# Early heads' out projection moved between the last head's steps, the first up block in other PSUM banks, and two last steps of a stage moved

## The chip, the cores and the metric

The kernel runs on one core of one Trainium2 chip. The metric is device time in microseconds (us), the median of three runs. Engine names: PE is TensorE (matmuls), PEld its weight loads, ACT is ScalarE, DVE is VectorE, POOL is GpSimd, SP is the engine that here only issues the weight loads.

## The reference, cut to what matters

The program is three transformer layers in float32 over 256 tokens of width 2048. Layer norms follow each part.

```python
# layer 0: pooling mixer, then MLP; layer 1: dilated attention, then MLP
h = pool_mixer(x, ...)  or  dilated_attention(x, w_qkv, w_out)
x = layer_norm(ALPHA * x + h, ...)
x = layer_norm(ALPHA * x + relu(x @ w_up)**2 @ w_down, ...)      # w_up 2048 x 8192
# dilated_attention: 3 groups x 8 heads; per head h the three groups' outputs are merged by a softmax
merged = einsum('gbsh,gbshe->bshe', wts, outs)                   # 256 x 1024, 8 heads of 128
h = merged @ w_out                                               # 1024 x 2048
# layer 2: a state-space mixer beside latent attention, then
a = depthwise_conv3(x @ w_up); gate, val = split(a)              # 2 x 5632
x = x + (silu(gate) * val) @ w_down
```

## The kernel before, in words

**Weights.** All weights stream from HBM in chunks of 128 x 2048 floats (1 MB). Four chunks are a quad; chunk s of a quad lives in slot s. SP loads slot s of quad q+1 into `raw` when slot s of quad q has been split (`lo_ready`). ACT rounds `raw` to `whi` (`hi1`, line 528), and DVE forms `wlo = raw - whi` (`lo1`, line 1028). PE needs both (`chunk(q, s)`), does three matmuls for each product (hi x hi, hi x lo, lo x hi) and raises `chunk_used`; ACT's `hi1` of the next quad's slot s waits for that. So each chunk goes SP, ACT, DVE, PE, and every engine follows an order written out by hand. A chunk is 48 matmuls of 256 columns (lines 1807 to 1809, up-type products) or 24 of 512 columns (lines 1855 to 1857, `rows_tile`, down-type products).

**PSUM.** Eight banks. `block_ps(b)` is banks 2b and 2b+1 (an up block: four 128 x 256 tiles); `down_ps(nb)` is banks 4, 5 or 6, 7 (one 512-column block of the output, one bank for each half of the tokens, tt = 0 and 1). DVE adds a finished block to `resid` (`add_rows`, line 1068, or `add_half`, line 1073) and takes its statistics (`block_stats`, line 1079).

**MLP stages (`mlp`, names mlp0 and mlp1).** 16 hidden blocks of 512. PE: `block_first` makes up block 0 into block_ps(0), then a loop of `up(g+1)` and `down(g)`; the last one is `down_last`, which does tt = 0 over all four slots and then tt = 1. All up blocks go to block_ps(0), so up(g+1) waits (`block_free`) for ACT's Relu of block g (line 646). For g = 0 that Relu stands in ACT's order behind the four `hi1` of the next quad, whose last one waits for `block_first` to end. ACT then squares (648) and rounds (654) the hidden block; DVE forms its low part (1189) behind four `lo1` and the rescale of `resid` (1159, 1168). Ahead of `block_first`, `turn_x` (line 1870) transposes the normalised rows into block_ps(0) to block_ps(3), and ACT's `x_piece` reads them (582, 584).

**Table jobs.** Beside mlp0, POOL makes 16 small table jobs (lines 1750 to 1782) for the third layer; PE's `ssm_tables(j)` (lines 1926 and 1931, banks 2 and 3) stands between up(j+1) and down(j), and the last, job 15, between down(14) and `down_last`. ACT copies the results and stores them (`table_out`, `inner_store`); POOL starts job j+1 when job j's stores and the next `compact` input have landed. `inner_store` waits for POOL's add (1781), which waits for `load_skip`'s transfer.

**The end of the attention stage.** PE runs q, k, v of head h in blocks of banks 0 to 3, with head h-1's steps in between: `scores` (2022, 2023, banks 4 to 6), `turn` (2030: nine transposes of the probabilities), `mix` (2038, 2041: 18 small matmuls into bank 7). Between scores and turn lie DVE's `shift` and `probs` (1396 to 1412) and ACT's `exps`; between turn and mix ACT's `copy_turned` (769); after mix ACT's `copy_head` (773) and DVE's `head_low` (1416). For the last head there are no further q, k, v products to put in between. After it comes the out projection: quad attn_out holds output blocks nb = 0, 1, each as two chunks (heads 0 to 3, then heads 4 to 7), quad attn_out+1 holds nb = 2, 3. The first waits for `head_low` of the last head.

**The ffn stage of layer 2.** 11 hidden blocks; per block two up quads (gate, value) and a down quad. DVE's `group` makes the convolution (1654), `hid = conv * sigmoid` (1672), then for the value half: an `add_down`, a `lo1`, the gated product `hid *= value` (1682), three more adds and `lo1`, and the low part of hid (1684). ACT rounds hid (998) behind the four `hi1` of the down quad. Before it may write `hid_hi` it waits for the down product of the block before.

Of the kernel before, what the change touches and what calls it, by code (L numbers as in the profile page):

```python
# [20 lines left out]
P = 128  # L21
T = 256
# [71 lines left out]
for _name, _n in (("mix0", 4), ("mlp0", 4), ("mix1", 4), ("attn2", 4), ("q", 1), ("kv", 1), ("ssm", 2), ("mla", 2), ("ffn2", 4)):  # L94
# [62 lines left out]
def build(nc, x_t, x_rows, gain_rows, weights, ssm_compact, ssm_skip, features, consts, dist_table, ssm_lam, positions, out):  # L157
    with ExitStack() as ctx:
# [362 lines left out]
        def _(act):  # L521
# [50 lines left out]
            def x_piece(name, y, p):  # L572

                n = 4 * TURNED[name] + p + 1
                gain, g0, bias, b0 = GAIN[name]
                if LO0[name] + p >= 2:
                    act.wait_ge(norm_lo, LO0[name] + max(0, p - 1))
                act.wait_ge(tok_turned, n)
                for i in range(4):
                    k = 4 * p + i  # L580
                    if bias is None:
                        ins = act.activation(y[:, p % 2, i, :], block_ps(p)[:, i, :], ACT.Copy, scale=fcol(gain, g0 + k))
                    else:
                        ins = act.activation(y[:, p % 2, i, :], block_ps(p)[:, i, :], ACT.Identity, scale=fcol(gain, g0 + k),
                                             bias=fcol(bias, b0 + k))
# [52 lines left out]
            def mlp(name, tables=False):  # L638
# [354 lines left out]

            def ffn_split(g):
                act.wait_ge(hidden_ready, g + (h0 + 1))
                if not (isinstance(g, int) and g == 0):
                    wait_used(act, g * 3 + (q0 + 1))
                act.activation(hid_hi[:], hid[:], ACT.Copy).then_inc(hidden_hi, 1)

            def group(g, q):  # L1000
# [15 lines left out]
            group(n - 1, q0 + 3 * n - 2)  # L1016
            for tt in range(2):
# [4 lines left out]
        def _(dve):  # L1022
# [641 lines left out]

            def group(g, q, adds):

# [6 lines left out]
                for s in range(1, SLOTS):  # L1673
                    lo1(q, s)
                conv_rest(g, 1)
                for s in range(SLOTS):
# [6 lines left out]
                dve.wait_ge(hidden_hi, g + (h0 + 1))  # L1683
                dve.tensor_tensor(hid_lo[:], hid[:], hid_hi[:].bitcast(F32), ALU.subtract).then_inc(hidden_lo, 1)  # L1684
            lo4(q0 + 1)
            group(0, q0 + 2, False)
            with dve.Fori(0, n - 2) as g:
# [3 lines left out]
                step.leave(n - 2)  # L1691
            group(n - 1, q0 + 3 * n - 2, True)

# [103 lines left out]
        def _(pe):  # L1797
# [50 lines left out]

            def rows_tile(o, s, tt, kts, xh, xl, first, last):


                t = slice(tt * P, tt * P + P)
                for j, k in enumerate(kts):
                    c = slice(j * 512, j * 512 + 512)
# [5 lines left out]
            def turn_x(name, src, sem_, value, n_free):  # L1860


                for tt in range(2):
                    for nb in range(4):
# [3 lines left out]
                        for i in range(4):  # L1868
                            c = slice(512 * nb + i * P, 512 * nb + i * P + P)
                            ins = pe.transpose(block_ps(nb)[:, i, tt * P:tt * P + P], src[:, tt, c], ccol("ident"))  # L1870
                        if tt == 1:
# [16 lines left out]
            def block_first(name, q, free):  # L1888

                pe.wait_ge(block_free, free)  # L1890
                pair_first(name, [block_ps(0)[:, s, :] for s in range(4)], 0, 2, lambda s: chunk(q, s))
                quad_tile(q, 0, 1, 1, 2)
                quad_tile(q, 0, 3, 3, 1)

# [9 lines left out]

            def down_last(q, u, hidden, hi, lo):
# [29 lines left out]
            def mlp(name, tables=False):  # L1935
                q0, b0, h0, n = QUAD[name], BLOCK[name], HIDDEN[name], FF // HID

                def up(g):
                    quad_block(g * 2 + (q0 - 1), 0, g + (b0 + 2))
# [10 lines left out]
                down_last(q0 + 2 * n - 1, UNITS[name] + 8 * (n - 1), h0 + n, last_hi, last_lo)  # L1950
                if tables:
# [121 lines left out]
            scores(N_HEADS - 1)  # L2073
            turn(N_HEADS - 1)
            mix(N_HEADS - 1, 1)
            pe.wait_ge(head_lo, 1 + N_HEADS)
            q, u = QUAD["attn_out"], UNITS["attn_out"]

            def head_rows(nb, tt, s):
                k0 = 4 * (s % 2)  # L2080
                return rows_tile(down_ps(nb)[:, tt, :], s, tt, range(k0, k0 + 4), heads_hi, heads_lo, s % 2 == 0, s % 2 == 1)
            for s in range(SLOTS):
                nb = s // 2
                chunk(q, s)
                if s % 2 == 0:
                    pe.wait_ge(down_free, u + 2 * nb - 2)
                head_rows(nb, 0, s)
                head_rows(nb, 1, s).then_inc(chunk_used, 1)
            for tt in range(2):
                for s in range(SLOTS):  # L2090
                    nb = 2 + s // 2
                    if tt == 0:
                        chunk(q + 1, s)
                        if s % 2 == 0:
                            pe.wait_ge(down_free, u + 2 * nb - 2)
                    ins = head_rows(nb, tt, s)
                    if tt:
# [200 lines left out]
            down_last(q0 + 3 * n - 1, UNITS["ffn"] + 8 * (n - 1), h0 + n, hid_hi, hid_lo)  # L2298

# [37 lines left out]
def pack_weights(i):  # L2337
# [35 lines left out]
    attn[:, :, 0:3] = qkv  # L2373
    parts += [attn.reshape(-1, P, CW), blocks(i["attn_w_out"][0]), mlp(i["mlp_w_up"][1], i["mlp_w_down"][1])]
    w = i["w_in_2"][0]
# [57 lines left out]
```

## Time and profile before

| | |
|---|---|
| median of 3 runs | 3462.59 us (3462.33 to 3462.66) |
| profiled execution, its own time | 3466.21 us |
| its span | 3464.4 us |
| mean granted TensorE clock | 0.977 of full |
| PE busy | 3293.8 us (95%) |
| DVE, ACT, POOL busy | 57%, 42%, 9% |
| chain that ended last | PE 89%, DVE 5%, ACT 3%, DMA 2%, issue 1% |

The span is the time from the first to the last instruction; the device time holds 1.8 us more around it. The chain that ended last is followed back from the last instruction, at each step to what released it: a share there is time that a shorter step would give back. In a timeline a row is a start, a duration, an engine, a line, what was written from what, and in brackets the idle time before it with the instruction that ended it. The modelled end of a matmul lies behind the start of the next one, so steps are measured from start to start.

### The profile page before, as it was taken

The page shows a single profiled execution, that of the slowest core. Times are in us where ns is not written, and L with a number is a line of the kernel's source. Part 1 is how long each engine was busy: PE and PEld are TensorE (multiplying, and loading weights), DVE is VectorE, ACT ScalarE, POOL GpSimd, SP SyncE. Part 2 cuts the span into 40 slices and gives each one's busy share as a digit, 9 for nine tenths or more (in the row PEclk, how much of TensorE's full clock was granted, in tenths as well). Part 3 has the DMA queues.
Part 4 walks back from the last instruction along what each step waited for, and adds up shares of the span by engine and source line. Part 5 has one row for each costly group of instructions (what it writes and reads, how often), then busy time and mean ns, then how long its engine had stood idle before and what let it go on. Part 6 is the DMA issues. An engine that isn't in the chain of part 4 may idle for free.

```text
span 3464.4 us, 54486 instructions
## 1 busy us (share of the span) xinstructions
PE 3293.8 (95%) x22368; PEld 3029.7 (87%) x22368; DVE 1970.0 (57%) x1709; ACT 1461.4 (42%) x1281; POOL 321.3 (9%) x474
## 2 busy tenths in 40 slices
PE   7899999999989999979999999979789999999998
PEld 6779899999879999969888889969667999999997
DVE  7756555555555444456555555567445666666656
ACT  4334444444444444434444434434553544444442
POOL 1301322333310000000000000006000000000000
PEclk9999999999999999999999999989899999999999
DMA  6345655555545444536555555535223555555552
GB/s 260 143 173 204 201 200 198 197 200 201 199 143 182 173 172 158 181 125 230 187 188 183 191 183 186 189 135 194 77 93 134 195 187 185 187 188 186 183 191 98
DMA packets 117688, 613.40 MB, mean 177 GB/s; under 512 B 14481, under 2 KB 45265, under 8 KB 47185
## 3 DMA queue, kind: packets, MB, share of 16 engines
q1 hardware_dynamic: 94640, 594.79, 48.3%
q10 hardware_dynamic: 22944, 17.10, 1.5%
q8 instruction: 82, 1.34, 0.2%
q14 instruction: 22, 0.17, 0.0%
HBM read 599.26 MB, written 12.58 MB: 177 GB/s over the span
## 4 chain that ended last, share of the span: by engine, by line
PE 89%; DVE 5%; ACT 3%; DMA 2%; issue 1%; POOL 0%; SPq 0%; ACTq 0%; DVEq 0%; POOLq 0%
PE ps L1807 17%; PE ps L1809 17%; PE ps L1808 17%; PE ps L1855 11%; PE ps L1856 11%; PE ps L1857 11%; DMA raw<-weights 1%; DVE wlo L1028 1%; ACT whi L528 1%; ACT y_mix L874 1%; PE ps L1931 0%; PE ps L2119 0%; PE ps L1846 0%; PE ps L2041 0%; DVE row_stats L1079 0%
## 5 line engine op out<-in xcount | busy, mean ns | idle before, releaser
L1028 DVE TENSOR_TENSOR wlo<-raw,whi 128x2048 fp32r<-128x2048 f32 (+2 forms) x572 | 1259.4, 2207 | 1099.0 <-ACT whi L528 1095.3
L528 ACT ACTIVATE whi<-raw 128x2048 fp32r<-128x2048 f32 (+2 forms) x572 | 1044.1, 1831 | 1624.6 <-PE ps L1809 977.7
L1807 PE MATMUL ps<-x_pair,whi 128*128 128x256 f32 x5104 | 1440.8, 282 | 56.8 <-DVE wlo L1028 32.6
L1809 PE MATMUL ps<-x_pair,wlo 128*128 128x256 f32 x5104 | 1432.9, 281 | 0.0
L1808 PE MATMUL ps<-x_pair,whi 128*128 128x256 f32 x5104 | 1432.5, 281 | 0.0
L1807 PEld LDWEIGHTS ps<-x_pair,whi 128*128 128x128 f32 x5104 | 966.3, 189 | 62.5 <-issue 52.9
L1809 PEld LDWEIGHTS ps<-x_pair,wlo 128*128 128x128 f32 x5104 | 966.9, 189 | 0.0
L1808 PEld LDWEIGHTS ps<-x_pair,whi 128*128 128x128 f32 x5104 | 965.1, 189 | 1.9
L1855 PE MATMUL ps<-whi,hid_hi 128*128 128x512 f32 x1312 | 520.0, 396 | 5.5 <-DVE hid_lo L1684 5.5
L1857 PE MATMUL ps<-whi,hid_lo 128*128 128x512 f32 x1312 | 518.5, 395 | 0.0
L1856 PE MATMUL ps<-wlo,hid_hi 128*128 128x512 f32 x1312 | 518.5, 395 | 0.0
L1068 DVE TENSOR_TENSOR resid<-resid,ps 128x1024 f32<-128x1024 f32 x171 | 208.7, 1221 | 198.7 <-PE ps L1857 195.7
L1855 PEld LDWEIGHTS ps<-whi,hid_hi 128*128 128x128 f32 x1312 | 246.5, 188 | 64.5 <-DVE hid_lo L1684 6.0
L1857 PEld LDWEIGHTS ps<-whi,hid_lo 128*128 128x128 f32 x1312 | 246.3, 188 | 60.4
L1856 PEld LDWEIGHTS ps<-wlo,hid_hi 128*128 128x128 f32 x1312 | 246.5, 188 | 58.6
L385 POOL TENSOR_TENSOR scan_room<-state,hop 128x64 f32<-128x64 f32 (+3 forms) x20 | 10.1, 503 | 1362.9 <-ACT state L862 1361.5
L1654 DVE SCALAR_TENSOR_TENSOR conv<-ps,feat,conv 128x255 f32<-128x255 f32 (+1 forms) x176 | 72.6, 475 | 2.7
L1773 POOL TENSOR_TENSOR b_four<-job_tmp 64x128 f32<-64x128 f32 x64 | 59.1, 924 | 0.0
L1781 POOL TENSOR_TENSOR inner_out<-inner_out,lag_out 128x256 f32<-128x256 f32 x16 | 11.8, 738 | 502.4 <-ACT lag_out L622 502.4
L1770 POOL TENSOR_TENSOR c_wide<-job_tmp 64x160 f32<-64x160 f32 x64 | 51.8, 810 | 4.9
L758 ACT ACTIVATE qkv_t<-ps 128x768 f32<-128x768 f32 x24 | 19.5, 811 | 74.6 <-PE ps L1809 74.6
L1855 PE MATMUL ps<-whi,x_pair 128*128 128x512 f32 x128 | 50.4, 394 | 0.0
(341 smaller groups left out, 2470.4 us busy)
## 6 DMA issues: line engine op xcount, KB each, us to landing
raw<-weights SPq DMA_DIRECT2D x539, 1024.0 KB, 4.8
read_tab<-read_tables SPq DMA_DIRECT2D x2, 3072.0 KB, 12.4
raw<-weights SPq DMA_DIRECT2D x8, 640.0 KB, 8.1
drive_tables<-drive_out ACTq DMA_DIRECT2D x16, 256.0 KB, 6.0
read_tables<-c_wide ACTq DMA_DIRECT2D x32, 128.0 KB, 5.9
drive_tab<-drive_tables SPq DMA_DIRECT2D x4, 1024.0 KB, 7.0
x_in<-x_t SPq DMA_DIRECT2D x4, 512.0 KB, 6.8
resid<-x_rows ACTq DMA_DIRECT2D x1, 2048.0 KB, 14.2
```

The costliest lines, as they stand in the source:

```text
L528: act.activation(whi[:, s, 0:width], raw[:, s, 0:width], ACT.Copy).then_inc(hi_ready, 1)
L1028: dve.tensor_tensor(wlo[:, s, 0:width], raw[:, s, 0:width], whi[:, s, 0:width].bitcast(F32), ALU.subtract).then_inc(lo_ready, 1)
L1068: return dve.tensor_tensor(r, r, ps[:, bank:bank + 2, :], ALU.add).then_inc(sem_, n)
L1654: ins = dve.scalar_tensor_tensor(out=o, in0=block_ps(half_)[:, nt, 0:T - lag], scalar=fcol("ffn_conv_w_2", i + tap * (2 * FF2 // P)), in1= ...
L1770: step(pool.tensor_tensor(wide[rows, e, :, :, 16 * g:16 * g + 16], a[rows], b[rows], ALU.add))
L1773: step(pool.tensor_tensor(b_four[rows, e, :, :, 16 * g:16 * g + 16], a[rows, :, STEP - 1:STEP, :].to_broadcast(same), b[rows, :, STEP - 1: ...
L1807: pe.matmul(o, w_hi, x_hi, start=first, stop=False)
L1808: pe.matmul(o, w_hi, x_lo, start=False, stop=False)
L1809: return pe.matmul(o, w_lo, x_hi, start=False, stop=last)
L1855: pe.matmul(o, xh[:, k, t], whi[:, s, c], start=first and j == 0, stop=False)
L1856: pe.matmul(o, xh[:, k, t], wlo[:, s, c], start=False, stop=False)
L1857: ins = pe.matmul(o, xl[:, k, t], whi[:, s, c], start=False, stop=last and j == 3)
```

## The change

- **Attention end.** The chunks of attn_out are packed in another order: slot 0 is block 0 with heads 0 to 3, slot 1 is block 1 with heads 0 to 3, slots 2 and 3 are the two with heads 4 to 7. PE runs slots 0 and 1 between the last head's `scores` and `turn`, heads 4 and 5 of slot 2 between `turn` and `mix`, head 6 behind `mix`, and then head 7 and slot 3. Blocks 0 and 1 now go to banks 0 to 3. DVE forms slots 0 and 1 of the next quad first and does its two add-and-statistics steps behind them.
- **First up block.** For mlp0 and mlp1 the transposed rows and the first up block swap block_ps(0) and block_ps(1): `block_first` writes block_ps(1), and up(1) writes block_ps(0) without waiting for the Relu of block 0. PE's loop is turned: its body is now tables and down(g), then up(g+2).
- **Last table job.** PE runs `ssm_tables(15)` between the tt = 0 and tt = 1 halves of `down_last`; ACT takes the standard deviation of the first token half before `table_out(15)`.
- **Last ffn block.** The gated product is formed directly behind the convolution, ACT rounds it before the four `hi1`, into buffers of its own (`end_hi`, `end_lo`), and DVE forms the low part behind the first `lo1`.

```diff
+TURNED_IN = {n: (1, 0, 2, 3) if n[:3] == "mix" else (0, 1, 2, 3) for n in TURNED}
...
+        end_hi = at("end_hi", 84, [P, 4, T], F32R)
+        end_lo = at("end_lo", 88, [P, 4, T], F32R)
...   ACT
-                row_sqrt(name, 0, eps)
+                if name != "mlp0":
+                    row_sqrt(name, 0, eps)
...
-                    act.activation(hid[:], block_ps(0), ACT.Relu).then_inc(block_free, 1)
+                    first = isinstance(g, int) and g == 0
+                    act.activation(hid[:], block_ps(1 if first else 0), ACT.Relu).then_inc(block_free, 1)
...
                 hi4(q0 + 2 * n - 1)
                 if tables:
+                    row_sqrt(name, 0, "ln_eps")
                     table_out(n - 1, True)
...   ACT, ffn group
                 conv_first(g, 1)
+                if last:
+                    ffn_split(g, True)
                 hi4(q + 1)
-                ffn_split(g)
+                if not last:
+                    ffn_split(g)
...   DVE, attention end
+            lo1(q + 1, 0)
+            lo1(q + 1, 1)
             for nb in range(2):
-                lo1(q + 1, 2 * nb)
-                lo1(q + 1, 2 * nb + 1)
-                wait_used(dve, q, 2 * nb + 1)
-                add_block(nb, 4 + 2 * nb, down_free, 2, u + 2 * nb + 2)
+                wait_used(dve, q, nb + 2)
+                add_block(nb, 2 * nb, down_free, 2, u + 2 * nb + 2)
+                lo1(q + 1, nb + 2)
...   DVE, ffn group
+                if last:
+                    value()
                 for s in range(SLOTS):
                     if adds:
                         add_down(q, s)
                     lo1(q + 1, s)
                     if s == 0:
-                        step.settle()
-                        dve.tensor_tensor(hid[:], hid[:], conv[:, 4:8, :], ALU.mult).then_inc(hidden_ready, 1)
+                        split(end_hi, end_lo) if last else value()
...   PE, down_last
                 for tt in range(2):
+                    if tt and tables:
+                        ssm_tables(JOBS - 1)
...   PE, mlp
-                with pe.Fori(0, n - 1) as g:
-                    up(g + 1)
-                    if tables:
-                        ssm_tables(g)
-                    down(g * 2 + (q0 + 2), g * 8 + UNITS[name], g + (h0 + 1))
-                if tables:
-                    ssm_tables(n - 1)
+                quad_block(q0 + 1, 0, b0 + 2)
+                with pe.Fori(0, n - 2) as g:
+                    rest(g)
+                    quad_block(g * 2 + (q0 + 3), 0, g + (b0 + 4))
+                rest(n - 2)
...   PE, attention end
+            head_rows(0, 0, 0, low)
+            head_rows(0, 1, 0, low).then_inc(chunk_used, 1)
+            chunk(q, 1)
+            pe.wait_ge(v_ready, 3 * N_HEADS)
+            head_rows(1, 0, 1, low)
+            head_rows(1, 1, 1, low).then_inc(chunk_used, 1)
             turn(N_HEADS - 1)
+            chunk(q, 2)
+            for tt in range(2):
+                head_rows(0, tt, 2, high[0:2])
             mix(N_HEADS - 1, 1)
+            for tt in range(2):
+                head_rows(0, tt, 2, high[2:3], 2)
             pe.wait_ge(head_lo, 1 + N_HEADS)
...
+            head_rows(0, 0, 2, high[3:4], 3)
+            head_rows(0, 1, 2, high[3:4], 3).then_inc(chunk_used, 1)
+            chunk(q, 3)
+            head_rows(1, 0, 3, high)
+            head_rows(1, 1, 3, high).then_inc(chunk_used, 1)
```

## Rows read from the trace of the kernel before

**Rows 1.** PE's waits by line and releaser: us in total, times, longest.
```profile
PE ps L1807 <- ACT hid L646: 6.2, 2, 3.1
PE ps L1855 <- DVE hid_lo L1684: 5.5, 1, 5.5
PE ps L1926 <- POOLq L1778: 5.4, 1, 5.4
```

**Rows 2.** PE's timeline, end of the attention stage: start, duration, engine, line.
```profile
1482.97 0.60 PE L2023 MATMUL ps<-qkv_t 128*128 128x256 f32 x2
1493.75 2.18 PE L2030 MATMUL ps<-const,score 128*128 128x128 f32 x9 [10.18 <-DVE score L1412]
1497.15 1.65 PE L2038 MATMUL ps<-prob_t,v_rows 128*128 128x128 f32 x6 [1.22 <-ACT prob_t L769]
...
1501.89 0.50 PE L1855 MATMUL ps<-whi,heads_hi 128*128 128x512 f32 x1 [0.93 <-DVE heads_lo L1416]
```

**Rows 3.** PE's timeline, the same two steps of an earlier head.
```profile
1104.62 1.15 PE L2030 MATMUL ps<-const,score 128*128 128x128 f32 x9
1105.53 0.37 PE L1807 MATMUL ps<-x_pair,whi 128*128 128x256 f32 x1
...
1122.57 0.83 PE L2038 MATMUL ps<-prob_t,v_rows 128*128 128x128 f32 x6
...
1124.58 0.38 PE L2016 MATMUL ps<-const,qkv_t 128*128 128x128 f32 x2
```

**Rows 4.** Timelines of ACT and DVE in the out projection.
```profile
1507.85 1.92 ACT L528 ACTIVATE whi<-raw 128x2048 fp32r<-128x2048 f32 x1 [6.47 <-PE ps L1857]
...
1509.80 2.29 DVE L1028 TENSOR_TENSOR wlo<-raw,whi 128x2048 fp32r<-128x2048 f32 x1 [7.96 <-ACT whi L528]
...
1517.61 1.22 DVE L1068 TENSOR_TENSOR resid<-resid,ps 128x1024 f32<-128x1024 f32 x1
1518.86 1.29 DVE L1079 BATCH_NORM_STATS2 row_stats<-resid 128x6 f32<-128x512 f32 x2
```

**Rows 5.** PE's timeline, mlp0: end of block_first to the second tables.
```profile
284.90 0.28 PE L1809 MATMUL ps<-x_pair,wlo 128*128 128x256 f32 x1
...
312.52 0.60 PE L1926 MATMUL ps<-const,b_wide 128*128 128x128 f32 x4
...
313.77 0.48 PE L1855 MATMUL ps<-whi,hid_hi 128*128 128x512 f32 x1
...
336.24 0.28 PE L1807 MATMUL ps<-x_pair,whi 128*128 128x256 f32 x1
...
358.86 0.60 PE L1926 MATMUL ps<-const,b_wide 128*128 128x128 f32 x4
```

**Rows 6.** PE's timeline, mlp1: last of block_first, first of down(0).
```profile
1579.35 0.28 PE L1809 MATMUL ps<-x_pair,wlo 128*128 128x256 f32 x1
...
1606.77 0.39 PE L1855 MATMUL ps<-whi,hid_hi 128*128 128x512 f32 x1
```

**Rows 7.** PE's timeline, mlp0: last of down(14), first transpose after down_last.
```profile
984.87 0.39 PE L1857 MATMUL ps<-whi,hid_lo 128*128 128x512 f32 x1
...
1016.57 0.60 PE L1870 MATMUL ps<-const,resid 128*128 128x128 f32 x4
```

**Rows 8.** Timelines of DVE and PE, last ffn block.
```profile
3411.30 1.22 DVE L1068 TENSOR_TENSOR resid<-resid,ps 128x1024 f32<-128x1024 f32 x1 [0.23 <-DVE conv L1654]
...
3425.49 0.40 PE L1857 MATMUL ps<-whi,hid_lo 128*128 128x512 f32 x1
...
3455.65 0.40 PE L1857 MATMUL ps<-whi,hid_lo 128*128 128x512 f32 x1
```

**Rows 9.** DMA issues of job 15's stretch: KB each, us to landing.
```profile
inner_out<-ssm_skip ACTq DMA_DIRECT2D x1, 128.0 KB, 4.0
```

**Rows 10.** Stretches: length, busy PE, PEld, DVE, ACT, POOL, granted PE clock, DMA.
```profile
3431.00:3436.00 5.00, 4.59 (x11) 3.65 (x12) 0.35 (x1) 0.00 (x0) 0.00 (x0) 0.52 0.00 0
...
2690.00:2720.00 30.00, 25.29 (x188) 23.23 (x187) 20.65 (x21) 19.47 (x26) 0.00 (x0) 1.00 0.61 213
```

More of the change, by code:

```diff
@@ L992, in gate, with ffn_split, group @@
                 act.activation(gate_sig[:], conv[:, 0:4, :], ACT.Sigmoid).then_inc(sig_ready, 1)
-            def ffn_split(g):
+            def ffn_split(g, last=False):
                 act.wait_ge(hidden_ready, g + (h0 + 1))
-                if not (isinstance(g, int) and g == 0):
+                if not last and not (isinstance(g, int) and g == 0):
                     wait_used(act, g * 3 + (q0 + 1))
-                act.activation(hid_hi[:], hid[:], ACT.Copy).then_inc(hidden_hi, 1)
-            def group(g, q):
+                act.activation(end_hi[:] if last else hid_hi[:], hid[:], ACT.Copy).then_inc(hidden_hi, 1)
+            def group(g, q, last=False):
                 conv_first(g, 0)
@@ L1663, in conv_rest, with group @@
                 dve.sem_inc(block_free, 1)
-            def group(g, q, adds):
+            def group(g, q, adds, last=False):
                 conv_rest(g, 0)
@@ L1675, in group, with value, split @@
                 conv_rest(g, 1)
+                def value():
+                    step.settle()
+                    dve.tensor_tensor(hid[:], hid[:], conv[:, 4:8, :], ALU.mult).then_inc(hidden_ready, 1)
+                def split(hi, lo):
+                    dve.wait_ge(hidden_hi, g + (h0 + 1))
+                    dve.tensor_tensor(lo[:], hid[:], hi[:].bitcast(F32), ALU.subtract).then_inc(hidden_lo, 1)
+                if last:
+                    value()
                 for s in range(SLOTS):
@@ L1680, in group @@
                     if s == 0:
-                        step.settle()
-                        dve.tensor_tensor(hid[:], hid[:], conv[:, 4:8, :], ALU.mult).then_inc(hidden_ready, 1)
-                dve.wait_ge(hidden_hi, g + (h0 + 1))
-                dve.tensor_tensor(hid_lo[:], hid[:], hid_hi[:].bitcast(F32), ALU.subtract).then_inc(hidden_lo, 1)
+                        split(end_hi, end_lo) if last else value()
+                if not last:
+                    split(hid_hi, hid_lo)
             lo4(q0 + 1)
@@ L1847, in norm, with rows_tile @@
                 ins.then_inc(norm_var, 1)
-            def rows_tile(o, s, tt, kts, xh, xl, first, last):
+            def rows_tile(o, s, tt, kts, xh, xl, first, last, j0=0):
                 t = slice(tt * P, tt * P + P)
-                for j, k in enumerate(kts):
+                for j, k in enumerate(kts, j0):
                     c = slice(j * 512, j * 512 + 512)
@@ L1890, in block_first @@
                 pe.wait_ge(block_free, free)
-                pair_first(name, [block_ps(0)[:, s, :] for s in range(4)], 0, 2, lambda s: chunk(q, s))
-                quad_tile(q, 0, 1, 1, 2)
-                quad_tile(q, 0, 3, 3, 1)
+                b = TURNED_IN[name][0]
+                pair_first(name, [block_ps(b)[:, s, :] for s in range(4)], 0, 2, lambda s: chunk(q, s))
+                quad_tile(q, b, 1, 1, 2)
+                quad_tile(q, b, 3, 3, 1)
             def down(q, u, hidden):
@@ L1903, in down, with down_last @@
                     ins.then_inc(chunk_used, 1)
-            def down_last(q, u, hidden, hi, lo):
+            def down_last(q, u, hidden, hi, lo, tables=False):
                 pe.wait_ge(hidden_lo, hidden)
                 for tt in range(2):
+                    if tt and tables:
+                        ssm_tables(JOBS - 1)
                     for s in range(SLOTS):
@@ L1936, in mlp, with rest @@
                 q0, b0, h0, n = QUAD[name], BLOCK[name], HIDDEN[name], FF // HID
-                def up(g):
-                    quad_block(g * 2 + (q0 - 1), 0, g + (b0 + 2))
+                def rest(g):
+                    if tables:
+                        pe.wait_ge(block_free, g + (b0 + 3))
+                        ssm_tables(g)
+                    down(g * 2 + (q0 + 2), g * 8 + UNITS[name], g + (h0 + 1))
                 block_first("mix" + name[-1], q0, b0 + 2)
+                quad_block(q0 + 1, 0, b0 + 2)
                 if tables:
                     pe.wait_ge(table_landed, 48)
-                with pe.Fori(0, n - 1) as g:
-                    up(g + 1)
-                    if tables:
-                        ssm_tables(g)
-                    down(g * 2 + (q0 + 2), g * 8 + UNITS[name], g + (h0 + 1))
-                if tables:
-                    ssm_tables(n - 1)
-                down_last(q0 + 2 * n - 1, UNITS[name] + 8 * (n - 1), h0 + n, last_hi, last_lo)
+                with pe.Fori(0, n - 2) as g:
+                    rest(g)
+                    quad_block(g * 2 + (q0 + 3), 0, g + (b0 + 4))
+                rest(n - 2)
+                down_last(q0 + 2 * n - 1, UNITS[name] + 8 * (n - 1), h0 + n, last_hi, last_lo, tables)
                 if tables:
@@ L2073, in _, with head_rows @@
             scores(N_HEADS - 1)
+            q, u = QUAD["attn_out"], UNITS["attn_out"]
+            def head_rows(nb, tt, s, ks, j0=0):
+                return rows_tile(ps[:, 2 * nb + tt, :], s, tt, ks, heads_hi, heads_lo, ks[0] == 0, ks[-1] == N_HEADS - 1, j0)
+            low, high = range(4), range(4, 8)
+            chunk(q, 0)
+            pe.wait_ge(v_ready, 3 * N_HEADS - 1)
+            head_rows(0, 0, 0, low)
[4 more added lines that the diff above has]
+            head_rows(1, 1, 1, low).then_inc(chunk_used, 1)
             turn(N_HEADS - 1)
+            chunk(q, 2)
+            for tt in range(2):
+                head_rows(0, tt, 2, high[0:2])
             mix(N_HEADS - 1, 1)
+            for tt in range(2):
+                head_rows(0, tt, 2, high[2:3], 2)
             pe.wait_ge(head_lo, 1 + N_HEADS)
[L2077 to L2088, printed above, removed]
+            head_rows(0, 0, 2, high[3:4], 3)
[3 more added lines that the diff above has]
+            head_rows(1, 1, 3, high).then_inc(chunk_used, 1)
             for tt in range(2):
                 for s in range(SLOTS):
[L2091 removed]
                     if tt == 0:
                         chunk(q + 1, s)
[L2094 to L2096 removed]
+                    ins = head_rows(2 + s // 2, tt, s, high if s % 2 else low)
                     if tt:
@@ L2297, in _ @@
                 down(g * 3 + (q0 + 4), g * 8 + UNITS["ffn"], g + (h0 + 1))
-            down_last(q0 + 3 * n - 1, UNITS["ffn"] + 8 * (n - 1), h0 + n, hid_hi, hid_lo)
+            down_last(q0 + 3 * n - 1, UNITS["ffn"] + 8 * (n - 1), h0 + n, end_hi, end_lo)
 def shape_constants():
@@ L2373, in pack_weights @@
     attn[:, :, 0:3] = qkv
-    parts += [attn.reshape(-1, P, CW), blocks(i["attn_w_out"][0]), mlp(i["mlp_w_up"][1], i["mlp_w_down"][1])]
+    parts += [attn.reshape(-1, P, CW), blocks(i["attn_w_out"][0])[[0, 2, 1, 3, 4, 5, 6, 7]], mlp(i["mlp_w_up"][1], i["mlp_w_down"][1])]
     w = i["w_in_2"][0]
```

10 lines of the change are left out of this document (5 added, 5 removed).

## The prediction, made before the changed kernel had run

> **What bounds the kernel now.** I read the page first: PE is busy 95% of the span and is 89% of the chain that ended last, with DVE, ACT and POOL at 57%, 42% and 9% (the table ahead). So time goes only where PE works less or stands still less. The change removes no matmul; it can only fill PE's pauses. The second view is therefore PE's waits. Four kinds of pause are touched. Three stand in one view [rows 1]: the first up block of each MLP waits for ACT's Relu (2 times 3.1 us), the last ffn block waits for DVE's low part (5.5), and the last table job for POOL (5.4). The fourth is the last head's chain, where the timeline shows 10.18, 1.22 and 0.93 us of standing [rows 2]. Together that is 6.2 + 5.5 + 5.4 + 12.3 = 29.4 us. The third view is the granted clock. Behind the ffn pause it is 0.52 of full for 5 us [rows 10], that is, the lower of the two levels, 1.2 GHz, after PE had done nothing for 5.5 us. A pause thus costs its length and a slow stretch behind it. So I don't sum waits; I measure each place from start to start and subtract what the same matmuls take elsewhere at full clock.
>
> **Unit prices at full clock**, from the loop of mlp0 [rows 5]: an up quad takes 358.86 - 336.24 = 22.62 us, a down quad 336.24 - 313.77 = 22.47 (0.234 per matmul, 5.6 per chunk), a table job 313.77 - 312.52 = 1.25.
>
> **Part 1, end of the attention stage.** Before: from the end of scores (1493.75 - 10.18 = 1483.57) to the first projection matmul (1501.89) are 18.3 us [rows 2]. In them lie turn and mix alone, which take 1105.53 - 1104.62 = 0.91 and 1124.58 - 1122.57 = 2.01 us in an earlier head [rows 3]. Excess: 15.4 us. After: does the moved work cover each wait, and is it there in time?
> - Scores to turn. Slots 0 and 1 are 48 matmuls, 11.2 us, from 1483.5 to 1494.7. The probabilities were ready at 1493.7, so the cover is 1 us too long, which costs nothing: PE is working. Banks 0 to 3 are free once ACT has copied the last v, which needs one short copy after scores.
> - Turn to mix. Turn ends at 1495.6; 12 matmuls of heads 4 and 5 last 2.8 us, and the copy in between was a 1.2 us wait plus PE's tail. Covered.
> - Mix to head 7. Six matmuls, 1.4 us, over a 0.93 us wait. Covered.
> - Head 7 of slot 2 ends at 1503.2, slot 3 at 1508.8, and slots 0 to 3 of the next quad are wanted at 1508.8, 1511.6, 1514.4 and 1517.2 (half a chunk each, tt = 0). ACT's rounding takes 1.92 us, DVE's low part 2.29, an add 1.22 and its statistics 1.29 [rows 4]. ACT starts behind copy_head at 1500.9; DVE has slot 0 at 1505.0 and slot 1 at 1507.2, adds block 0 until 1509.7, slot 2 at 1511.9. Slot 3 is freed by PE at 1508.9, rounded by 1511.0; DVE adds block 1 until 1514.3 and has slot 3 at 1516.5. This is the tightest: 0.7 us before PE wants it.
>
> So nothing waits. The first long matmul behind short ones lasts 0.48 us against 0.40 for another [rows 5, 8]; I take 0.1 for each such change, and there are four more: 15.4 - 0.4 = 15.0 us gained. Bounds: 10.0 if each of DVE's two adds with statistics (2.5 us) ends up in front of PE, 15.4 if nothing does. I take 15.0, since each deadline is met on paper.
>
> **Part 2, first up block.** Before, mlp0: the last matmul of block_first starts at 284.90 and tables begin at 312.52 [rows 5]. Without the wait it is 284.90 + 0.12 + 22.62 = 307.64: 4.9 us. In mlp1: 1606.77 - (1579.35 + 0.12 + 22.62) = 4.7 us [rows 6]. Of this 3.1 is the wait and the rest is slow matmuls behind it. What is late next? down(0) is now wanted 4.9 us earlier, and its hidden block stands on DVE behind four low parts and four rescale steps; the down chunks stand behind it. Counted from the end of block_first: the last rounding and low part 1.92 + 2.29, four rescale steps of the same shape taken at 2.29 each, the hidden low part at an add's 1.22, the first down chunk 2.29 [durations from rows 4], together 16.9 us, against 22.6 for the up quad. 5.7 us of cover remain. The Relu itself is still done 3 us after block_first, long before the tables use its banks. The swapped transposes are as many and as long as before. I take 9.6 us; bounds 6.2 (the waits alone) and 9.6.
>
> **Turned loop.** 14 instead of 15 rounds per MLP, with the jump between up and down. Before, the jump stood between down and up. The mlp0 loop shows no gap there: 22.47 us for 96 matmuls, of 0.234 each, up to the first matmul of the next round [rows 5]. I take 0. Bounds 0 and 3 us, below. The Trainium skill (Advanced Engine Details and Errata, Control Flow Timing) puts a compare-and-branch at about 108 ns; were all 28 jumps open, that alone would be an estimated 3 us. It speaks for a small price, and the trace shows none. The extra wait ahead of each table job was met long before, at the loop's own up block.
>
> **Part 3, last table job.** Before: from the end of down(14), 984.87 + 0.23, to the first transpose at 1016.57 are 31.5 us [rows 7]. The work is 22.47 + 1.25 = 23.7. Gain 7.75 us. POOL's job was ready 5.4 us after PE stood there [rows 1]; now PE comes 11.2 us later, so 5.8 us of cover remain. Given back: ACT now holds row_sqrt, the skip load, the copies, and inner_store, which waits for that load and POOL, in front of the attention stage's first hi1. That load took up to 4.0 us [rows 9], but earlier it was issued ahead of need, and now it starts only after the square root. ACT is free some 4 to 6 us after row_sqrt. In the first case DVE's first lo1 loses nothing; in the second it and the last adds come up to 1.6 us late. I take 7.7; bounds 6.1 and 7.75.
>
> **Part 4, last ffn block.** Before: 3425.49 + 0.23 to 3455.65 + 0.23 are 30.2 us [rows 8]; the work is 22.47. Excess 7.7. After: the gated product starts where the add started, 3411.30, ACT rounds by 3413.6, then the first hi1 by 3415.5, lo1 by 3417.8, low part by 3418.9, against 3425.7 when PE wants it. Next is the second add: it ends at 3420.1 instead of 3417.0, and slot 3 of down(9) wants its banks at 3420.2. I charge 0.1. All four chunks of the last quad are in time. Gain 7.6; bounds 6.5 (one further DVE step, 1.1 us, in front) and 7.7.
>
> **Sum.** 15.0 + 9.6 + 7.7 + 7.6 = 39.9 us. The profiled execution took 3466.21 (span 3464.4), so it would take 3426.3. The runs' median is 3.6 lower; I carry the difference over: 3462.6 - 39.9 = 3422.7 us.
>
> **Rivals.**
> - *The chunks come late.* The margins of 0.7 us (part 1), 0.1 (part 4) and ACT's longer queue (part 3) fail. For it: DVE and ACT get the new steps in front of chunks. Against: the durations are the same throughout the trace. Cost 5 + 1.6 + 1.1 = 7.7: 3430.4 us. Chance 0.12.
> - *Only the waits go, the clock stays.* The slow stretches come back elsewhere, because every later pause moves. In the tail before ffn the clock was 1.00 although PE stood there, while it fell behind the ffn pause [rows 10]; which pauses are followed by a slow stretch is thus not given by the code. Gain 29.4 alone: 3433.2 us. Against: five pauses are gone, and what no longer exists can't be followed by one. Half of it, or as much the other way, lies within my range. The Trainium skill (TensorE: Matmul & The Clock Gate, Part 1) has the activity count run free of the kernel, so that the number of slow matmuls varies; that is this rival's reason, and it gives no sign. Chance 0.12.
> - *Slower, by the turned loop.* If the jump between up and down opens a bubble on PE, it is paid 28 times. It cancels the gain at 39.9 / 28 = 1.4 us a round and makes the kernel slower by 0.2% from 1.7; at 2 us it is 3422.7 + 56 = 3478.7. Against: no bubble at the old place, and the weights and hidden blocks are there in either case. Chance 0.02.
> - *The wait moves instead of going*, in several places at once (PE held by ACT's copy of v, by POOL, by the adds): gain under 7 us, about 3458. No row speaks for it. Chance 0.02.
>
> **How the numbers follow.** The forecast has 0.72, by itself 3416 to 3429 (the bounds of parts 1 to 4 above; below, some later slow stretches that vanish). The range 3415.5 to 3431 takes in the late chunks and leaves out most of the clock rival. A measurement of this kernel tells about 0.2%, 7 us, from no change. Faster: 0.72 + 0.12 + 0.12 = 0.96; same 0.02; slower 0.02.
>
> **What would show it.** In PE's waits the rows for L646, L1684, L1778 and the three of the last head are gone. Right if turn and mix last 0.9 and 2.0 us there, the time from block_first's last matmul to down(0) is 22.7 us in mlp1, down_last of mlp0 with its tables 23.7, that of ffn 22.5. Wrong if PE waits for wlo in the second out-projection quad, for L1068 at slot 3 of down(9), or for L1068 and L1028 behind down_last of mlp0; if a gap stands at the loop's jump; or if the mean clock stays at 0.977 instead of rising to about 0.98.

## The result, and the profile after

The changed kernel takes 3427.88 us (median of 5 runs, 3425.14 to 3430.48), the kernel before 3462.66 beside it. The ratio, taken over the single runs, is 0.9891, 95% interval 0.9880 to 0.9901; the two medians alone give 0.9900. The predicted time was 3422.7, the range 3415.5 to 3431.0, so the time lies within it, 5 us above the forecast. The profiled execution took 3430.48 us, 35.7 less than the one before, where 39.9 was predicted. The sum came out roughly right, but two stretches that no term of it covers moved by 8 and by 6 us in opposite directions. That is the lesson of this case.

First, the head of the page of the changed kernel: busy time with share and count, the shares of the chain, and the queue that fetches instructions (packets, MB, share).

```profile
span 3428.7 us, 54490 instructions
...
PE 3285.4 (96%) x22368; PEld 3025.8 (88%) x22368; DVE 1968.9 (57%) x1709; ACT 1461.2 (43%) x1281; POOL 323.3 (9%) x474
...
q8 instruction: 87, 1.43, 0.2%
...
PE 90%; DVE 5%; ACT 3%; DMA 1%; issue 1%; SPq 0%; POOL 0%; DVEq 0%; ACTq 0%; POOLq 0%
```

PE went from 95% to 96%, and the mean granted clock from 0.977 to 0.982. Next, PE's waits over the whole span (total, times, longest).

```profile
PE ps L1826 <- issue: 12.5, 5, 3.1
...
PE ps L1827 <- issue: 4.3, 2, 2.5
...
PE ps L1826 <- ACT qkv_t L764: 1.7, 1, 1.7
```

The three rows of [rows 1] (Relu 6.2, ffn's low part 5.5, POOL 5.4) have no successor, nor have the three waits of the last head. But the second row is new: twice PE stood "for issue", that is, for nothing that the profile shows, on a line that had no wait at all before (L1808 there). The third row is one of two pauses that the kernel before had too, and the other of the two now counts in the first row, which was 10.9 us in 4 waits before. Both belong to the same story.

The end of the attention stage, PE's timeline, beside [rows 2]:

```profile
1491.98 0.40 PE L1876 MATMUL ps<-whi,heads_lo 128*128 128x512 f32 x1
1492.21 1.14 PE L2053 MATMUL ps<-const,score 128*128 128x128 f32 x9
1493.11 0.48 PE L1874 MATMUL ps<-whi,heads_hi 128*128 128x512 f32 x1
...
1495.76 0.39 PE L1876 MATMUL ps<-whi,heads_lo 128*128 128x512 f32 x1
1495.99 0.83 PE L2061 MATMUL ps<-prob_t,v_rows 128*128 128x128 f32 x6
1496.66 1.50 PE L2064 MATMUL ps<-prob_t,v_rows 128*128 128x128 f32 x12
1497.92 0.48 PE L1874 MATMUL ps<-whi,heads_hi 128*128 128x512 f32 x1
```

No brackets: turn takes 0.90 us, mix 1.93, as in an earlier head [rows 3], and matmuls run up to each and on behind it.

The first up block, beside [rows 5, 6]: the last matmul of `block_first`, the tables, down(0) and the next up block of mlp0, then the same first and third steps of mlp1.

```profile
287.05 0.28 PE L1828 MATMUL ps<-x_pair,wlo 128*128 128x256 f32 x1
...
309.78 0.60 PE L1948 MATMUL ps<-const,b_wide 128*128 128x128 f32 x4
...
311.03 0.48 PE L1874 MATMUL ps<-whi,hid_hi 128*128 128x512 f32 x1
...
333.51 0.28 PE L1826 MATMUL ps<-x_pair,whi 128*128 128x256 f32 x1
...
1561.63 0.28 PE L1828 MATMUL ps<-x_pair,wlo 128*128 128x256 f32 x1
...
1584.36 0.40 PE L1874 MATMUL ps<-whi,hid_hi 128*128 128x512 f32 x1
```

309.78 - 287.05 = 22.73 us and 1584.36 - 1561.63 = 22.73: an up quad at full clock and nothing else. The down quad takes 22.48, as before.

The last table job and the last ffn block, beside [rows 7, 8]:

```profile
982.13 0.40 PE L1876 MATMUL ps<-whi,hid_lo 128*128 128x512 f32 x1
...
993.56 0.60 PE L1948 MATMUL ps<-const,b_wide 128*128 128x128 f32 x4
...
1006.10 1.04 PE L1889 MATMUL ps<-const,resid 128*128 128x128 f32 x8
...
3397.50 0.39 PE L1876 MATMUL ps<-whi,hid_lo 128*128 128x512 f32 x1
...
3419.90 0.39 PE L1876 MATMUL ps<-whi,end_lo 128*128 128x512 f32 x1
```

The first pair is 23.97 us apart (31.70 before), the second 22.40 (30.16 before).

**Where the time went.** Stretches from the start of one PE matmul to the start of another, in us of each profiled execution:

| stretch | before | after | difference |
|---|---|---|---|
| start of the kernel to turn of mix0 | 252.1 | 254.3 | +2.1 |
| to the first tables (first up block, mlp0) | 60.4 | 55.5 | -4.9 |
| mlp0's loop, `down_last` and last table job | 704.1 | 696.3 | -7.7 |
| attention's first matmul to the last head's scores | 458.4 | 466.5 | **+8.1** |
| to turn of mix1 (attention's end) | 63.9 | 48.0 | -15.8 |
| mlp1's first matmul to down(0) | 51.5 | 47.3 | -4.2 |
| mlp1's loop | 683.5 | 683.5 | 0 |
| latent attention and state-space mixer | 344.8 | 339.2 | -5.6 |
| down products of the ffn | 661.0 | 653.2 | -7.8 |

The rest is alike. The edited places give back 40.4 us. The attention loop, which was not edited, takes 8.1 of it.

**The attention loop.** PE's timeline of the changed kernel at the loop's two jumps back:

```profile
1182.38 0.28 PE L1828 MATMUL ps<-x_pair,wlo 128*128 128x256 f32 x1
1184.37 0.38 PE L1826 MATMUL ps<-x_pair,whi 128*128 128x256 f32 x1 [1.71 <-ACT qkv_t L764]
...
1185.52 0.28 PE L1826 MATMUL ps<-x_pair,whi 128*128 128x256 f32 x1
1188.27 0.38 PE L1827 MATMUL ps<-x_pair,whi 128*128 128x256 f32 x1 [2.47 <-issue]
...
1303.84 0.38 PE L1826 MATMUL ps<-x_pair,whi 128*128 128x256 f32 x1 [1.94 <-issue]
...
1305.00 0.41 PE L1826 MATMUL ps<-x_pair,whi 128*128 128x256 f32 x1
1307.20 0.58 PE L1827 MATMUL ps<-x_pair,whi 128*128 128x256 f32 x1 [1.79 <-issue]
```

The same places of the kernel before:

```profile
1192.50 0.28 PE L1809 MATMUL ps<-x_pair,wlo 128*128 128x256 f32 x1
1194.47 0.38 PE L1807 MATMUL ps<-x_pair,whi 128*128 128x256 f32 x1 [1.70 <-ACT qkv_t L758]
...
1308.95 0.38 PE L1807 MATMUL ps<-x_pair,whi 128*128 128x256 f32 x1 [1.84 <-ACT qkv_t L758]
```

Before, PE stood once at each jump. After, it stands, runs ten matmuls, and stands again. Behind 1307.20 a matmul takes 0.21 us instead of 0.12: from 1307 to 1312 us the granted clock was 0.52, the lower of its two levels.

What differs is where the loop's instructions lie. In the built programs PE has 4985 instructions ahead of this loop before and 5593 after, since turning the loop of mlp0 wrote 608 more of them out. One round is 1938 instructions in both. Of these the trace shows 1908 between the two jumps of the kernel before, 954 matmuls and as many weight loads (stretch, length, busy PE, PEld, DVE, ACT, POOL, granted clock, DMA share, GB/s):

```profile
1194.40:1308.90 114.50, 112.64 (x954) 112.14 (x954) 51.19 (x44) 48.18 (x50) 0.00 (x0) 1.00 0.48 167
```

The instruction queue fetches blocks of 1.43 MB / 87 = 16.4 KB, and at the 64 bytes that an instruction has in the built program these are 256 instructions. After each jump PE gets through the first 22 instructions of the round (two for registers, then the ten matmuls with their weight loads) and stands. If that is a block's end, the loop's first instruction stands 234 into a block, and with 608 instructions fewer ahead of it, it stood 138 into one before.

The Trainium skill (Runtime: NRT & Kernel Launch, Instruction fetch mechanics) has 16 KiB blocks, sequential prefetch, and a stall where a taken branch leaves the window. The traces agree: a packet of the instruction queue starts within 1.2 us of the beginning of each of the four pauses (at 1181.47, 1185.92, 1300.71 and 1304.79 us), where in the rest of this loop they mostly come some 15 us apart. The page gives no price, and the traces do: 1.7 to 1.9 us for the target's block, 1.8 to 2.5 for the next where the first runs out at once. The kernel before jumps back 37 times in its other loops, whose rounds have 592 to 981 instructions, and not one of these jumps leaves a gap; in the changed kernel no instruction packet starts between 348.0 and 970.9 us, while the loop of mlp0 runs.

### The profile page after: what moved, and what is told of

Its sections match the earlier page's. It is cut to its first block, busy times and chain, and to the rows that moved or that the text cites. A ratio compares the mean times of both kernels' runs of the same rounds, so it can differ in the third digit from the quotient of the medians.

```text
span 3428.7 us, 54490 instructions
## 1 busy us (share of the span) xinstructions
PE 3285.4 (96%) x22368; PEld 3025.8 (88%) x22368; DVE 1968.9 (57%) x1709; ACT 1461.2 (43%) x1281; POOL 323.3 (9%) x474
## 3 DMA queue, kind: packets, MB, share of 16 engines
q8 instruction: 87, 1.43, 0.2%
## 4 chain that ended last, share of the span: by engine, by line
PE 90%; DVE 5%; ACT 3%; DMA 1%; issue 1%; SPq 0%; POOL 0%; DVEq 0%; ACTq 0%; POOLq 0%
PE ps L1826 17%; PE ps L1828 17%; PE ps L1827 17%; PE ps L1874 12%; PE ps L1875 12%; PE ps L1876 12%; DMA raw<-weights 1%; DVE wlo L1037 1%; ACT whi L531 1%; ACT y_mix L880 1%; PE ps L1953 0%; PE ps L2150 0%; PE ps L1865 0%; DVE row_stats L1088 0%; ACT y_rms L585 0%
## 5 line engine op out<-in xcount | busy, mean ns | idle before, releaser
L1874 PE MATMUL ps<-whi,hid_hi 128*128 128x512 f32 x1280 | 507.1, 396 | 0.0
L1875 PE MATMUL ps<-wlo,hid_hi 128*128 128x512 f32 x1280 | 505.8, 395 | 0.0
L1876 PE MATMUL ps<-whi,hid_lo 128*128 128x512 f32 x1280 | 505.8, 395 | 0.0
```

The costliest lines, as they stand in the source:

```text
L1874: pe.matmul(o, xh[:, k, t], whi[:, s, c], start=first and j == 0, stop=False)
L1875: pe.matmul(o, xh[:, k, t], wlo[:, s, c], start=False, stop=False)
L1876: ins = pe.matmul(o, xl[:, k, t], whi[:, s, c], start=False, stop=last and j == 3)
```

## The experiments

Each ratio stands against the kernel before, run again beside the experiment: its median was 3464.3 us beside experiments 1 to 4, 3465.8 beside 5 to 8 and 3467.2 beside 9 and 10. A time is best read against its own. A stretch comes from one profiled execution of each kernel.

**1. The kernel before with its loop moved.** No other edit:

```
-            with pe.Fori(0, N_HEADS // 2 - 1) as i:
+            with pe.bass.Fori(0, N_HEADS // 2 - 1, engines=[pe.engine], head_slot={pe.engine: 234}) as i:
```

> The kernel before, with one edit: the first instruction of PE's attention loop is placed at slot 234 of a block of 256 instructions, where the trace puts it in the changed kernel (22 instructions run behind the jump, then PE stands for 2.47 and 1.79 us). By counting instructions ahead of the loop it stood at about slot 164 before. Theory A (PE's instruction fetch at the loop's jump): the attention loop grows by about 8 us as in the changed kernel (458.5 to about 466 us from its first matmul to the last scores), two new pauses of about 2 us, total about 3470 us. Theory B (the 8 us come from shifted weight transfers or from where slow clock stretches happen to fall): the loop stays at 458.5, total within 2 us of 3462.7.

3472.88 us, ratio 1.0026 [1.0016, 1.0037]: some 9 us slower. The stretch of the loop went from 458.4 to 463.6, which is 5.2 us and not 8; the start of the kernel (2.1), the first up block (2.7) and the end of attention (2.1) were longer too, with no edit in them, and later stretches shorter. PE's waits in the loop's stretch:

```profile
PE ps L1808 <- issue: 4.8, 2, 2.7
PE ps L1807 <- ACT qkv_t L758: 3.3, 2, 1.7
```

The changed kernel's second pause came, at both jumps, with nothing but the loop's place. So neither banks, nor chunk order, nor ACT's new order made it.

**2 and 3. Part 2 alone, and with its loop put back.** The first up block in its other banks and the turned MLP loop, the rest as before. In the second kernel `head_slot` is 164, where by my count (582 instructions more, where the built program has 608) the loop stood before; it stood at 138. What the comparison needs holds for both places: they are far from a block's end.

```
+                block_first("mix" + name[-1], q0, b0 + 2)
+                quad_block(q0 + 1, 0, b0 + 2)
...
+                with pe.Fori(0, n - 2) as g:
+                    rest(g)
+                    quad_block(g * 2 + (q0 + 3), 0, g + (b0 + 4))
+                rest(n - 2)
```

> Part 2 alone on the kernel before: first up block in banks of its own, PE's MLP loop turned, last table job still ahead of down_last. The turned loop unrolls one more round ahead of the attention loop, so this is the part that moves it by 582 instructions. Theory A: mlp0 gives 4.9 us, mlp1 4.2 to 4.7, the attention loop takes 8 back: net about -1 us, 3461 to 3462. Theory B: about -9.3 us, 3453.4.

> Part 2 alone, with the attention loop's first instruction put back at slot 164. Theory A: the loop is at 458.5 us again and the full 9.3 us show: 3453.4. Theory B: as part 2 alone without the placement, since nothing but the place of PE's code differs.

3460.03 us, ratio 0.9989 [0.9980, 0.9999], and 3452.90, ratio 0.9967 [0.9956, 0.9978]. The loop stretch was 466.5 and 456.8. Waits in it, first of part 2 alone:

```profile
PE ps L1810 <- issue: 4.5, 2, 2.4
PE ps L1809 <- issue: 1.9, 1, 1.9
PE ps L1809 <- ACT qkv_t L760: 1.4, 1, 1.4
```

then with the loop put back:

```profile
PE ps L1809 <- ACT qkv_t L760: 3.2, 2, 1.7
```

The up blocks gained their 9 us in both (55.5 and 47.3 us in the table's stretches). Where the loop happened to land took 8.0 us of it away. The whole kernels differ by 7.1 us, and the intervals of their ratios don't touch.

**4. The changed kernel with its loop on a block boundary** (`head_slot` 0).

> The changed kernel with the attention loop's first instruction at slot 0 of a fetch block. Theory A: both second pauses (2.47 and 1.79 us) go and with them the slow clock behind them, 4.3 + 3.4 = 7.7 us: 3420.2. The first pause of each jump (1.7 us) stays. Theory B: no change, 3427.9 give or take 3.

3421.55 us, ratio 0.9879 [0.9862, 0.9895]; the stretch fell from 466.5 to 457.1. The whole time alone would not show it, since the interval of the ratio overlaps with that of the changed kernel (0.9880 to 0.9901); the pauses do. One per jump is left, again put down to ACT:

```profile
PE ps L1826 <- ACT qkv_t L764: 3.4, 2, 1.8
```

**5, 6, 7. Parts 1, 3 and 4 alone.**

```
# part 1: PE between scores, turn and mix of the last head
+            chunk(q, 0)
+            pe.wait_ge(v_ready, 3 * N_HEADS - 1)
+            head_rows(0, 0, 0, low)
...
# part 3: between the token halves of down_last
+                    if tt and tables:
+                        ssm_tables(JOBS - 1)
...
# part 4: ACT, ahead of the four hi1
+                if last:
+                    ffn_split(g, True)
```

> Part 1 alone on the kernel before: only the end of the attention stage is changed. By the working of the prediction 15.0 us less; the stretch from the last scores to the first transpose of the next norm shrinks from 63.87 us to 48.0, as in the whole change. Since this part adds PE instructions only behind the attention loop, the loop's 458.5 us stay. Rival (part of the 15.85 us measured there is due to the other parts, for instance weights that arrive earlier): 52 us or more in that stretch.

> Part 3 alone: the last table job between the halves of down_last, ACT's square root ahead of it. Expected 7.7 us less; from the first tables to the first transpose 704.05 us become 696.3. The number of PE instructions ahead of the attention loop is unchanged, so the loop stays at 458.5 us. Rival (the skip load behind the square root holds ACT and the last adds): 697.9 us there, 6.1 less in all.

> Part 4 alone: gated product, rounding and low part of the last ffn block earlier and in buffers of their own. Expected 7.6 us less; from the first down product of ffn to the last matmul 660.97 us become 653.2 to 653.3. Rival (DVE's second add, three steps later, holds slot 3 of down(9)): 654.3 and a wait of PE for L1068.

| part | time | ratio | its stretch, before and alone |
|---|---|---|---|
| 1 | 3449.00 | 0.9958 [0.9944, 0.9973] | 63.9, 48.0 |
| 3 | 3456.89 | 0.9979 [0.9970, 0.9989] | 704.1, 696.3 |
| 4 | 3459.41 | 0.9983 [0.9974, 0.9993] | 661.0, 653.2 |

Each stretch has the length it has in the full change, so in these places the parts don't touch each other. The whole kernel's time shows the same less sharply: against the 3465.8 us beside them the three gained 16.8, 8.9 and 6.4 us. One of my expectations was missed: the attention loop, unedited and at its old place in all three, did not stay at 458.5 us but took 456.5, 454.7 and 457.5. So this stretch moves by up to 4 us from kernel to kernel without an edit in it, and the mixer's, below, by more. The 8.1 us of the changed kernel's loop are clear of that, but known only to within some us.

**8. Boundary and hint together.** The changed kernel, with the back jump told to PE's prefetcher ahead of time:

```
-            with pe.Fori(0, N_HEADS // 2 - 1) as i:
+            with pe.bass.Fori(0, N_HEADS // 2 - 1, engines=[pe.engine], head_slot={pe.engine: 0}, hint_back_edge=True) as i:
```

> The changed kernel, the attention loop's first instruction at slot 0 and a branch prefetch hint for its closing branch at the top of each round. Theory A (the first pause of each jump, 1.7 us in both kernels and put down to ACT's qkv copy, is a fetch as well): 2 times 1.7 us go and with them a slow stretch, some 3.4 to 5 us below the kernel with slot 0 alone: 3417. Rival (that pause is the wait for ACT's copy, as its row says): no change, 3421.5.

3411.62 us (3410.26 to 3420.66), ratio 0.9858 [0.9841, 0.9874]: 16 us under the changed kernel, with an interval that does not touch its own, and some 5 us under what I had expected. The stretch is 451.5 us, 15.1 less than in the changed kernel, and the row of the qkv copy is gone from the loop. PE's and ACT's timelines show why that row had been misread. PE just behind the jump (the round's first matmul starts at 1177.35):

```profile
1177.47 0.28 PE L1827 MATMUL ps<-x_pair,whi 128*128 128x256 f32 x1
1177.59 0.28 PE L1828 MATMUL ps<-x_pair,wlo 128*128 128x256 f32 x1
...
1178.18 0.28 PE L1827 MATMUL ps<-x_pair,whi 128*128 128x256 f32 x1
```

ACT at the same time:

```profile
1177.55 0.81 ACT L764 ACTIVATE qkv_t<-ps 128x768 f32<-128x768 f32 x1 [3.74 <-PE ps L1828]
```

PE runs matmul after matmul while the copy is being made, so it never needed it. In the kernel before the copy merely ended in the middle of the pause (PE stood from 1192.8 to 1194.5):

```profile
1192.81 0.81 ACT L758 ACTIVATE qkv_t<-ps 128x768 f32<-128x768 f32 x1 [3.74 <-PE ps L1809]
```

**9 and 10. The kernel before with boundary and hint; the changed kernel with the hint alone** (no `head_slot`).

> The kernel before, with PE's attention loop begun on a block boundary of its instructions and its back jump hinted, nothing else. Theory (each back jump waits for the loop's first instructions to be fetched, whatever the profile names beside the pause): PE's two pauses put down to ACT's qkv copies (3.5 us) go, as they did in the changed kernel, and the stretch from the first matmul of attention to the last head's scores falls from 458.4 to 451.5 us: 3462.7 - 7 = about 3456, with the place of the slower clock free to move it by 3 either way. So of the 16 us between the changed kernel and its hinted form at least 8 are what the change had itself lost, and only about 7 were there to be had before. Rival (those pauses are waits for the qkv copies, and the hinted form was fast because its clock was lucky): the pauses stay and the stretch is 456 to 458.

> The changed kernel with the hint on the back jump alone, the loop's first instruction left where the change put it, 22 instructions ahead of a block's end. If the hint brings in only the block of the jump's target: the first pause of each jump (1.7 and 1.9 us) goes, the second (2.5 and 1.8 us, behind the 22 instructions) stays or gets shorter, and the stretch of the attention loop is 457 to 463 against 466.5 of the changed kernel and 451.5 with the head on a boundary as well: total 3419 to 3425. If the hint brings in what follows too, both pauses go and the stretch is about 452, total about 3412: then the place of the head matters only without the hint. Rival (the hint does nothing, the place alone did it): 466 and 3428.

The kernel before: 3459.65 us, ratio 0.9979 [0.9970, 0.9988], that is, 7.6 us under the 3467.2 beside it, where 7 were forecast; the stretch is 451.5, as in experiment 8. The qkv row is gone, the others stayed:

```profile
PE ps L1807 <- DVE x_pair L1121: 3.1, 1, 3.1
PE ps L1807 <- DVE wlo L1028: 1.7, 1, 1.7
```

So of the 15.1 us that experiment 8 took out of the loop, 7.0 had been in the kernel before and 8.1 were the change's own loss. The changed kernel with the hint alone: 3419.07 us, ratio 0.9857 [0.9841, 0.9873], stretch 454.8. Its loop has kept this:

```profile
PE ps L1826 <- issue: 1.1, 2, 0.6
```

That is between my two cases: the hint hides the target's block entirely and the next one down to 0.5 and 0.6 us. The whole times don't separate this kernel from that of experiment 8, whose ratio and interval are the same within 0.0001; the stretch and the pauses do. The instruction queue's rows are those of the pages of the changed kernel on a boundary (85 packets, experiment 4), with the hint alone (86), and with both:

```profile
q8 instruction: 67, 1.10, 0.1%
```

With both, 20 packets fewer are fetched than in the changed kernel (and 63 against 82 in the kernel before). The missing ones are those of the loop. In the changed kernel the queue has these from 1156 to 1402 us, over both jumps and most of the last two rounds:

```profile
q8 instruction: 21, 0.34, 0.6%
```

With both, it has none at all from 1156 to 1402 us, and none from 1175 to 1421 us in experiment 9. So the hint alone only fetches ahead of time, while the hinted loop on a boundary is not fetched again. Why both are needed for that no run here shows. The Trainium skill (the same section) gives PE an instruction memory of 2048, into which the 1938 would fit. That is eight blocks, and the round lies across eight from a boundary and across nine from 234, which would be a reason for the boundary; but no hinted loop at a third place was run, and without the hint the loop on a boundary (experiment 4) is fetched anew all the same.

## Why the prediction was right in time and wrong in a step

**The step that failed** is "Turned loop. 14 instead of 15 rounds per MLP, with the jump between up and down ... I take 0. Bounds 0 and 3 us". Its own question was answered rightly: mlp1's loop takes 683.51 us before and after, and 333.51 - 311.03 = 22.48 us leave no gap at a jump. But I asked only what the turned loop costs where it stands. Writing rounds out moves every later instruction of PE, and 8.1 us came up in another loop, 178 and 298 us behind the last matmul of mlp0. Experiment 1 shows that the place alone brings the second pauses (with 5.2 us of the 8), experiments 2, 3 and 4 that putting the loop elsewhere takes them away. The third rival named a jump that opens a bubble, but in the MLP loops and 28 times over (14 rounds jump back 13 times, so it would have been 26); it was the attention loop's, twice. The trace before did hold the sign: two pauses of 1.7 and 1.8 us exactly at the two jumps. I took them, where I saw them at all, for waits on ACT.

**Part 1**: 15.0 predicted, 63.87 - 48.02 = 15.85 measured. All seven deadlines held, the tightest with 0.7 us on paper too. 192 matmuls of 0.234 with turn 0.9 and mix 2.0 are 47.8, so of the 0.4 charged for changes of shape 0.2 was paid. Another 0.3 is that before, the out projection's own matmuls took 45.17 us instead of 44.9, slow ones behind the old pause, beyond the point to which I measured. The last 0.4 is that I counted from the modelled end of the last score (1483.57) and not from its start (1483.19).

**Part 2**: 4.9 in mlp0 was 4.88. In mlp1 the stretch from `block_first`'s last matmul shrank by 27.42 - 22.73 = 4.69, as predicted (4.7), while `block_first` itself took 24.6 instead of 24.1 us. That is not the change's doing: with parts 1, 3 and 4 alone the whole stretch is 52.1 to 52.2 us, also longer than the 51.5 of the kernel before. The hidden block was in time, as the sum of 16.9 against 22.6 said.

**Part 3**: 7.7 was 7.73. ACT's longer queue cost nothing: from the first transpose of mlp0's rows to attention's first matmul are 8.16 us before and after. **Part 4**: 7.6 was 7.75. None of the margins, 0.1 us in one case, was missed, so the rival of late chunks falls. So does the rival that only the waits go: the four places gave 40.4 us, not 29.4, slow stretches included. The forecast's upper end, though, was not what the text made it: the low bounds of the four parts add to 28.8 us, which is 3433.8 and not 3429.

**A term not in the sum**: the mixer, in which nothing was edited, took 5.6 us less. Windows over it (length, busy PE, PEld, DVE, ACT, POOL, granted clock, DMA share, GB/s), first of the kernel before:

```profile
2305.00:2650.00 345.00, 292.31 (x1977) 264.57 (x1978) 185.80 (x285) 165.56 (x227) 52.07 (x116) 0.91 0.37 135
```

and of the changed one:

```profile
2282.60:2621.80 339.20, 287.22 (x1976) 260.11 (x1977) 185.72 (x285) 165.52 (x227) 52.06 (x116) 0.92 0.37 137
```

The same matmuls were busy 5.1 us longer at a lower clock. In the other ten kernels with this same code the stretch took from 339.2 to 343.3 us, without order: with the kernel before's loop merely hinted 341.5, with part 1 alone 342.2, with part 2 alone 340.2. The start of the kernel moves likewise from 251.5 to 254.4. No edit explains where these slow stretches of the clock fall, and I count it as luck, which had the better of it by 3.5 us (5.6 less 2.1). Without it the profiled gain would be 32 us, of which the parts are 40.4 and the loop -8.1. What makes a slow stretch fall here or there stays open.

## What to carry to other kernels

Whoever unrolls, turns or lengthens code moves all later code of that engine in its fetch blocks: count the instructions ahead of each long loop, and look at what stands behind each jump, in stages that the edit does not touch as well. A pause at a loop's first instruction, whatever releaser is named beside it, is to be tried as a fetch first. Hinting the back jump and starting the loop on a boundary is a line of code, and took 7.0 us out of the loop in one kernel and 15.1 in the other. For the edits proper, measuring from start to start and subtracting the same matmuls at full clock sized each within 0.9 us, where summing waits alone would have missed a quarter.

## What the runs showed that I had not expected

- A loop of 1938 instructions on PE pays 1.4 to 2.0 us at each jump back in every kernel without the hint, and 1.8 to 2.7 us more if its first instruction stands 22 ahead of a block's end. The MLP loops, with some 600 a round, and that of the ffn stage, with 981, pay nothing.
- With the pauses go slow stretches: the changed kernel's loop lost 15.1 us to pauses of 7.9 us in all.
- The releaser beside a pause is inferred. Here it named ACT's copy, which ended within the pause, at both jumps of the kernel before, and the row went when the fetch was hinted. In four kernels (the changed one and those with part 2, 3 or 4 alone) one of these two pauses stands under "issue" instead, at 1.9 to 2.0 us and with the same code at the jump: the name changes and the pause stays.
